# Modulation product of a 1-core transformer kernel: weighted sums on VectorE, partition sums by a column of ones on PE

## The reference, cut to what matters

```python
def swiglu(x, w_in, w_out):
    gate, up = jnp.split(x @ w_in, 2, axis=-1)
    return (jax.nn.silu(gate) * up) @ w_out

def modulate(h, shift, scale):
    return h * (1 + scale[:, None, :]) + shift[:, None, :]
```

## Time and profile before

| | us |
|---|---|
| median of 3 runs | 1971.3 |
| lowest and highest | 1969.5, 1971.41 |
| the profiled execution | 1973.3 |
| its span | 1971.1 |

### The profile page before, as it was taken

The page is one execution under the profiler, slowest core; times in us unless marked ns, Lnnn a source line. Parts: engine busy times, 40 slices in busy tenths (PEclk is TensorE's granted clock), DMA queues, the critical chain, the costliest instruction groups (busy, mean ns, idle before and its releaser), DMA issues.

```text
span 1971.1 us, 25483 instructions
## 1 busy us (share of the span) xinstructions
PE 1911.1 (97%) x10311; PEld 1589.6 (81%) x10311; DVE 1143.9 (58%) x1369; ACT 953.7 (48%) x1399; POOL 118.0 (6%) x182
## 2 busy tenths in 40 slices
PE   7999999999999999999999999899999999989997
PEld 5777788777777777877877777899889987878996
DVE  5554776645475445845556556675565557565554
ACT  4444563544454434544454445554554456544442
POOL 1400001000010000000010000000200001000000
PEclk9999999999999999999999999999999999999999
DMA  9867543876757675554586664444455545234552
GB/s 297 260 220 252 171 150 99 295 235 221 240 196 244 226 243 197 190 176 164 167 294 224 223 235 147 165 172 170 153 172 190 189 150 176 86 117 149 194 173 84
DMA packets 234100, 379.77 MB, mean 193 GB/s; under 512 B 12040, under 2 KB 152720, under 8 KB 233984
## 3 DMA queue, kind: packets, MB, share of 16 engines
q1 hardware_dynamic: 231200, 369.69, 56.2%
q0 software_dynamic: 2448, 8.33, 1.6%
q10 hardware_dynamic: 336, 0.14, 0.0%
HBM read 377.06 MB, written 1.05 MB: 192 GB/s over the span
## 4 chain that ended last, share of the span: by engine, by line
PE 89%; DVE 6%; ACT 2%; issue 1%; DMA 1%; POOL 1%; SPq 0%; POOLq 0%; ACTq 0%; DVEq 0%
PE ps L450 22%; PE ps L452 22%; PE ps L451 22%; PE ps L1134 4%; PE ps L1136 4%; PE ps L1137 4%; PE ps L460 4%; PE ps L577 2%; DVE w_lo L2047 2%; PE ps L627 1%; PE ps L1277 1%; PE ps L609 1%; PE ps L1256 1%; DVE xt_lo L2063 1%; ACT arena L1512 1%
## 5 line engine op out<-in xcount | busy, mean ns | idle before, releaser
L2047 DVE TENSOR_TENSOR w_lo<-raw,w_hi 128x1024 fp32r<-128x1024 f32 x602 | 719.9, 1227 | 241.7 <-ACT w_hi L1402 238.7
L1402 ACT ACTIVATE w_hi<-raw 128x1024 fp32r<-128x1024 f32 x602 | 614.6, 1056 | 258.0 <-PE ps L452 181.2
L450 PE MATMUL ps<-w_hi,xt_hi 128*128 128x512 f32 x1280 | 510.1, 398 | 16.2 <-DVE xt_lo L2197 11.8
L452 PE MATMUL ps<-w_hi,xt_lo 128*128 128x512 f32 x1280 | 500.4, 391 | 0.0
L451 PE MATMUL ps<-w_lo,xt_hi 128*128 128x512 f32 x1280 | 500.0, 391 | 0.0
L450 PE MATMUL ps<-w_hi,ht_hi 128*128 128x512 f32 x784 | 314.6, 401 | 5.9 <-DVE ht_lo L2225 2.7
L451 PE MATMUL ps<-w_lo,ht_hi 128*128 128x512 f32 x784 | 306.9, 391 | 0.0
L452 PE MATMUL ps<-w_hi,ht_lo 128*128 128x512 f32 x784 | 306.7, 391 | 0.0
L450 PEld LDWEIGHTS ps<-w_hi,xt_hi 128*128 128x128 f32 x1280 | 242.4, 189 | 68.1 <-issue 19.2
L452 PEld LDWEIGHTS ps<-w_hi,xt_lo 128*128 128x128 f32 x1280 | 242.3, 189 | 51.3
L451 PEld LDWEIGHTS ps<-w_lo,xt_hi 128*128 128x128 f32 x1280 | 242.6, 190 | 48.3 <-issue 1.2
(11 more groups left out here) (273 smaller groups left out, 1365.8 us busy)
## 6 DMA issues: line engine op xcount, KB each, us to landing
raw<-mlp_w_dram SPq DMA_DIRECT2D x192, 512.0 KB, 4.4
raw<-ffn_w_in_dram SPq DMA_DIRECT2D x176, 512.0 KB, 5.8
arena<-ada_w_dram SPq DMA_DIRECT2D x96, 512.0 KB, 6.5
raw<-ffn_w_out_dram SPq DMA_DIRECT2D x88, 512.0 KB, 4.5
raw<-odd_w_in_dram SPq DMA_DIRECT2D x48, 512.0 KB, 4.9
raw<-attn_w_qkv_dram SPq DMA_DIRECT2D x24, 512.0 KB, 4.9
raw<-even_w_in_dram SPq DMA_DIRECT2D x22, 512.0 KB, 4.7
raw<-ple_w_gate_dram SPq DMA_DIRECT2D x16, 512.0 KB, 4.5
```

The source lines that it names most:

```text
L450: pe.matmul(dst, a_hi, hi, start=start, stop=False)
L452: return pe.matmul(dst, a_lo, hi, start=False, stop=stop)
L1402: act.activation(w_hi[:, slot, c], raw[:, slot, c], ACT.Copy).then_inc(S(f"hi{slot}"), 1)
L2047: TT(w_lo[:, slot, c], raw[:, slot, c], w_hi[:, slot, c].bitcast(F32), ALU.subtract).then_inc(S(f"lo{slot}"), 1)
```

## The change

The slabs of the modulation weights are cut differently: 128 x 4 x 512 (half of the contraction, 512 columns) instead of 128 x 8 x 256, still 1 MB and 12 in a run. DVE now does the weighting: for each k and each of the two variants, `scalar_tensor_tensor` multiplies a 128 x 512 piece by a scalar for each partition (`s_col`) and adds it to a running sum `ada_sum` in `tmp` (the first k is a `tensor_scalar`). That is 8 DVE instructions a slab (`ada_part`, in two halves of 4), 384 in the program. After two slabs PE adds over the partitions (`ada_columns`): 8 float32 matmuls, each with a 128 x 128 piece of the sum as weights and a column of ones as the one moving column, which write straight into the columns that `ada_t` wants. There are 6 such groups in a run, after `up` in steps 1, 3, 5, 7 and 9, and one at the end in the place of `ada_turn`. `ada_product`, `ada_turn` and `ada_row` go; `ada_cols` becomes one copy.

DVE does slab 0 after the split that follows `gated(0)`, slabs 1 and 2 both in step 0, and slab i+2 in step i. SP loads slab 2 right behind slab 1, ahead of s5, and this load waits until DVE has done slab 0 (`ada_mac`).

```diff
...
@@ -344,13 +345,13 @@
             def ada_load(run, i):
 
-                g = ADA_STEPS * run + i
+                g = ADA_STEPS * run + (0, 1, 3, 4, 5, 6, 7, 8, 9, 10, 11, 2)[i]
                 if g >= 2:
 
-                    sp.wait_ge(S("ada_prod"), g - 1)
-                w = ada_slab(run, i)
+                    sp.wait_ge(S("ada_mac"), 8 * (g - 1))
+                w = ada_slab(run, g % ADA_STEPS)
...
                     ada_load(run, i + 1)
-                ada_load(run, FFN_STEPS)
+                    if i == 0:
+                        ada_load(run, FFN_STEPS)
                 load(wide(wo, 2 * FFN_STEPS - 2))
...
-            def ada_product(g):
...
-                for k in range(KT):
-                    q = 32 * (k % 4)
-                    last = pe.matmul(ps[q:q + 32, 7, 0:256], s_pad[:, k, 22 - 2 * i:54 - 2 * i], ada_raw[:, g % 2, k, :],
-                                     start=i == 0 and k < 4, stop=i == ADA_STEPS - 1 and k >= 4,
-                                     tile_position=(0, q), skip_group_check=True)
+            def ada_columns(group):
+
+                pe.wait_ge(S("ada_mac"), 16 * (group + 1))
+                for t in range(4):
+                    for v in range(2):
+                        c = 8 * (group % 6) + 2 * t + v
+                        last = pe.matmul(ps[:, 7, c:c + 1], ada_sum[:, group % 2, v, t * P:(t + 1) * P], ones[:],
+                                         start=True, stop=True)
                 last.then_inc(S("ada_prod"), 1)
...
                 for i in range(FFN_STEPS - 1):
                     hidden("f_", base + i, 2)
                     up(4, "f_up0")
-                    ada_product(ada + i + 1)
+                    if i % 2:
+                        if i == 1 and run:
+
+                            pe.wait_ge(S("ada_cols"), run)
+                        ada_columns(groups + i // 2)
...
-                ada_product(ada + FFN_STEPS)
...
-                ada_turn(run)
+                ada_columns(groups + 5)
...
-            def ada_row(run):
-                act.wait_ge(S("ada_prod"), ADA_STEPS * (run + 1))
-                act.activation(ada_rows[:], ps[:, 7, 0:256], ACT.Copy).then_inc(S("ada_row"), 1)
...
+            def ada_part(g, half):
+
+                if half == 0 and g % 2 == 0 and g >= 4:
+
+                    dve.wait_ge(S("ada_prod"), g // 2 - 1)
+                if half == 0:
+                    dve.wait_ge(S(f"ada_in{g % 2}"), 32 * (g // 2 + 1))
+                for j in (2 * half, 2 * half + 1):
+                    k = 4 * (g % 2) + j
+                    for v in range(2):
+                        to, w = ada_sum[:, g // 2 % 2, v, :], ada_raw[:, g % 2, j, :]
+                        n["ada"] += 1
+                        if k:
+                            dve.wait_ge(S("ada_mac"), n["ada"] - 2)
+                            ins = dve.scalar_tensor_tensor(to, w, s_col[:, v, k:k + 1], to, ALU.mult, ALU.add)
+                        else:
+                            ins = dve.tensor_scalar(to, w, s_col[:, v, k:k + 1], None, ALU.mult)
+                        ins.then_inc(S("ada_mac"), 1)
...
+                ada = ADA_STEPS * run
                 gated(base, out0)
                 split()
+                for half in range(2):
+                    ada_part(ada, half)
                 for i in range(FFN_STEPS - 1):
+                    slabs = (1, 2) if i == 0 else (i + 2,)
+                    ada_part(ada + slabs[0], 0)
                     ht_low(i)
                     split()
+                    ada_part(ada + slabs[0], 1)
                     split()
+                    for g in slabs[1:]:
+                        for half in range(2):
+                            ada_part(ada + g, half)
                     gated(base + i + 1)
...
```

More of the change, by code:

```diff
@@ L143, in build @@
         pt_lo = sb("pt_lo", [P, 2, SEQ], F32R)
-        s_pad = sb("s_pad", [P, KT, 54])
+        s_col = sb("s_col", [P, 2, KT])
+        ones = sb("ones", [P, 1])
         arena = sb("arena", [P, 15360])
@@ L226, in ada_slab @@
             w = rows(T["ada_w_2"][run // 2])
-            return w[:, :, bass.ds((run % 2) * 12 * 256 + i * 256, 256)]
+            return w[:, 4 * (i % 2):4 * (i % 2) + 4, bass.ds((run % 2) * 6 * 512 + i // 2 * 512, 512)]
         EVEN_CHUNKS = ((2048, 512), (2560, 256), (512, 512), (0, 512), (1024, 512), (1536, 512))
@@ L274, in build @@
         onorm_b = small[:, 128:256]
-        ada_rows = region(5120, 256)
-        ada_raw = region(10240, 2, KT, 256)
+        ada_raw = region(10240, 2, 4, 512)
+        ada_sum = cut(tmp[:], 2, 2, 512)
         pool_w = region(2560, KT, 256)
@@ L684, in ffn @@
                 base = FFN_STEPS * run
-                ada = ADA_STEPS * run
+                groups = ADA_STEPS // 2 * run
                 if out0 == 0:
@@ L1593, in ffn @@
                     act.activation(pt_hi[:], cut(bank(5), 2, SEQ), ACT.Copy).then_inc(S("pt_hi"), 1)
-                ada_row(run)
                 if run == 3:
@@ L2033, in _ @@
             ring = Ring()
-            n = {k: 0 for k in ("x", "x2", "sq", "epi", "pj", "ple", "step", "pool", "y", "mlp")}
+            n = {k: 0 for k in ("x", "x2", "sq", "epi", "pj", "ple", "step", "pool", "y", "mlp", "ada")}
             TT = dve.tensor_tensor
@@ L2181, in pool_add @@
                 dve.wait_ge(S("pool_y"), n["y"] + 1)
+                if n["y"] in (2, 3):
+                    dve.wait_ge(S("c_upd"), n["y"] - 1)
                 n["y"] += 1
                 c = slice(512 * half, 512 * half + 512)
-                t = cut(tmp[:], 2, MT, 512)[:, half, m]
+                if upd == "c_upd":
+                    t = arena[:, 8736 + 544 * half:8736 + 544 * half + 512]
+                else:
+                    t = cut(tmp[:], 2, MT, 512)[:, half, m]
                 TT(t, bank(b), gate[:, c], ALU.mult).then_inc(S("p_free"), 1)
@@ L2199, in ada_cols @@
             def ada_cols(run):
[L2201 to L2206, removed]
+                dve.wait_ge(S("ada_prod"), 6 * (run + 1))
+                dve.tensor_copy(ada_t[:, 2 * ADA_STEPS * run:2 * ADA_STEPS * (run + 1), :].rearrange("p t v -> p (t v)"),
+                                ps[:, 7, 0:48]).then_inc(S("ada_cols"), 1)
+            def ada_part(g, half):
[11 more added lines that the diff above has]
+                            ins = dve.scalar_tensor_tensor(to, w, s_col[:, v, k:k + 1], to, ALU.mult, ALU.add)
+                        else:
+                            ins = dve.tensor_scalar(to, w, s_col[:, v, k:k + 1], None, ALU.mult)
+                        ins.then_inc(S("ada_mac"), 1)
             def ffn(run, out0=4):
@@ L2276, in _ @@
             dve.wait_ge(S("silu_c"), 1)
-            dve.wait_ge(S("s_zero"), 1)
-            sil = small[:, 0:16].rearrange("p (v k) -> p k v", v=2)
-            dve.tensor_copy(s_pad[:, :, 22:24], sil).then_inc(S("s_set"), 1)
+            dve.memset(ones[:], 1.0)
+            step(dve.tensor_copy(s_col[:].rearrange("p v k -> p (v k)"), small[:, 0:16]))
             (s0, u0), (s1, u1) = ring.take(), ring.take()
@@ L2859, in _ @@
             step(pool.memset(minus_half[:], -0.5))
-            pool.memset(s_pad[:], 0.0).then_inc(S("s_zero"), 1)
             token_scale()
```

16 lines of the change are left out of this document (2 added, 14 removed).

## The result

The changed kernel takes 2001.9 us in the median, from 2001.7 to 2002.4; the kernel before 1970.4 beside it. The ratio is 1.016, with a 95% interval from 1.0143 to 1.0178: **slower by 31.5 us**, where 32.7 were forecast, and inside the range. The span grew from 1971.1 to 2000.3 us, less than the medians did, since the profiled execution before was 2.9 us over its median. Ratios here are estimated from all executions of both kernels and not from the two medians, so the two can differ by up to 0.001.

A forecast was written before the change was run, and what follows sets the result against it. PE, busy 97% of the span, was taken to set the pace. PE's account -5.5, step 0's DVE wait +29.4 and the clock +8.8 sum to +32.7 us, giving a median of 2004.0 us, range 1984 to 2019.

The forecast's parts named there:

- The term that decides, step 0: Step 0 of each run: 24 new DVE instructions ahead of gated(1) make PE wait at hidden(1), together 29.4 us lost.
- Its parts: Step 0's loss by run: 7.3 us in run 0, 7.8 in runs 1 and 2, 6.5 in run 3.
- PE's account: PE's own work over all runs: modulation products removed against column groups added, -5.5 us in sum.
- The clock term: Behind the four waits at hidden(1), PE falls to half clock: 4 x 2.2 = 8.8 us lost.
- It fits, so a delay of 2.6 us reaches nobody: Steps 1 to 9: DVE's 13.6 us fit in PE's 16.9 or 18.7, with split slabs a step ahead; no loss.
- PE's account alone: Rival: DVE gets through step 0 before PE reaches hidden(1), leaving only -5.5 us, 1965.8 us; chance 0.07.
- product 1 of each run: Modulation product in step 0, 1.21 us; its removal was counted inside step 0's term, not among the 38 products gained.
- the 1.0 us of run 3: Gain from removing product 0 in run 3, where a gate row stands behind it; counted inside step 0's term.

The follow-up runs named there:

- experiment 1: The changed kernel with slab 2 summed on DVE behind gated(1), SP's order as it is: 1990.3 us, ratio 1.0099.
- experiment 2: The changed kernel with slab 2 loaded behind s5 and s6, DVE's order as it is: 1998.1 us, ratio 1.0141.
- experiment 3: The changed kernel with slab 2 both summed behind gated(1) and loaded behind s5 and s6: 1979.1 us, ratio 1.0043.
- experiment 4: As experiment 3, with the second half of slab 1 also summed behind gated(1): 1977.9 us, ratio 1.0038.
- experiment 6: The changed kernel with no split or gated behind more than 4 sums (except s6's split), loads mostly in the earlier kernel's order: 1967.2 us, ratio 0.9987.
- experiment 11: The changed kernel with unused extra matmuls right behind step 0's own PE work, 54 in run 0, 40 in the others: 1998.7 us, ratio 1.0139.
- experiment 9: As experiment 6, with POOL's small loads and rope tables in run 0 started after up of step 3, not step 0: 1960.1 us, ratio 0.9945.
- experiment 5: The changed kernel with 34 unused extra matmuls of 384 columns on PE ahead of hidden(1) in each run: 2003.8 us, ratio 1.0173.

## Why the prediction was right

- **The term that decides, step 0, held:** +29.7 us measured, +29.4 forecast. Experiments 1 to 4 show its cause: with both orders turned and half a slab more moved, run 1's step 0 falls to 17.6 us. Most of it belongs to DVE's queue; the load's order counts for 3.8 us alone, and for 11.1 once DVE's is mended (1990.3 - 1979.1); DVE's order counts for 11.6 alone and 19.0 once the load's is mended.
- **Its parts were less even than forecast.** Run 1 lost 7.1 (7.8 forecast), run 2 6.8 (7.8), since s5 reached ACT 8.6 us after slab 2's issue and not 9.8. Run 3 lost 6.6 (6.5). Run 0 lost 9.1 (7.3): two errors that cancel in the sum. In run 0, slab 2's six sums took longer than in run 1, where the row above has 4.06:

```profile
51.22 5.63 DVE L2210 SCALAR_TENSOR_TENSOR tmp<-arena,s_col,tmp 128x512 f32<-128x512 f32 x6
```

- **PE's account held.** A group is 1.78 us (1.79 forecast), nine steps of experiment 6 gain 4.0 (3.7), and a pair of steady steps went from 36.11 to 35.46. Behind `hidden(1)`, runs 1 to 3 came out 0.7, 1.5 and 0.7 better than by account and clock together.
- **The clock was the mis-sized term:** 4 x 2.2 = 8.8 us forecast, 2.0 + 1.9 + 1.3 + 0 = 5.2 by experiment 11. The price of one loss held in runs 1 and 2. But run 3's step 1 lost less, and in run 0 the slow stretch lay under late loads, which made step 1 there 2.5 us longer by themselves. The runs show three losses of 1.3 to 2.0 us in the place of four of 2.2.
- **That the sum came within 1.2 us of the median's change is partly luck.** The clock term was 3.6 too large. In run 0's stretch behind `hidden(1)` the late loads took 2.5 us where 2.2 were put down to the clock. At the end of run 0 the clock stayed at 1.00 behind a wait of 3.11 us, where before it had been 0.70 and 0.73 over 6 us behind one of 2.68, which the account of that stretch did not hold.
- **"It fits, so a delay of 2.6 us reaches nobody" was the wrong step.** It did no harm to this forecast, because a long wait at `hidden(1)` lets every load catch up. Take that wait away and step 1 waits instead: 28 us of it in run 0, and the 1965 expected of experiment 4 missed by 13. Experiment 9 names the cause, POOL's stretch in run 0, which the prediction did not look at: its sum over DVE was one over averages, and loads had a fixed latency in it.
- **PE's account alone** was priced too low as a rival: without a wait at `hidden(1)` product 1 of each run and the 1.0 us of run 3 are gained too, -5.5 - 4 x 1.21 - 1.0 = -11.3. So it is luck that experiment 6, with the order mended, has 1967.2 beside the rival's 1965.8: its step 1 of run 0 still loses 6.5 us. Freed of POOL's work as well (experiment 9), 9.6 us are measured beside the 11.3.

Open stays how much of step 1's 28 us in run 0 is POOL's hold on DVE and how much its loads; experiment 9 moves both.

## What to carry to other kernels

Price the new work on an engine with room not by its share of busy time but in the one step where it piles up, ahead of the instruction that the bounding engine waits for. Put filler work behind what others wait for and in small pieces, and move the loads' order with it: either alone gave back 12 or 4 us, both 23. And cost a TensorE instruction with few moving columns at its weight load (0.111 us for 128 x 128 float32 here). Two single traces can differ by 1 to 3 us in a stretch because the clock fell behind a wait in one and not in the other, so look at the granted clock before putting such a difference down to the kernel.

## What the runs showed of the hardware

**SP's loads nearly stand still for 7 to 8 us, some 7 us after POOL starts its loads of tables** (2 to 512 KB each). The kernel before in slices of 1 us from 28 us on (share of the DMA engines in tenths, then GB/s), POOL's loads issued from 41.8 to 45.2 us:

```profile
DMA  0001999988999999999990009200899999999999
GB/s 0 0 0 24 291 311 376 348 264 233 345 384 373 369 382 372 350 348 377 371 61 0 10 22 2 0 0 8 324 372 397 339 374 392 404 381 354 353 349 347
```

Between 48 and 56 us hardly a byte moves, though SP has issued loads that have not landed: those of 40.5 to 47.2 us take up to 18.6 us to land. In experiment 9, where POOL issues them from 77.6 us on, the hole lies at 84 to 91 us. What in those loads does it was not tried.

**DVE is slower beside POOL.** In run 0, six sums take 5.63 us instead of 4.06, 0.94 instead of 0.68 each. In step 1 of run 0 four take 3.31 us beside POOL (experiment 6) and 2.73 with POOL's work moved away (experiment 9), two halves of a split 2.60 and 2.35. The Trainium skill, "SBUF — State Buffer", section "SBUF: two separate sides", says that a DVE instruction with two inputs in SBUF and a GpSimd instruction that reads SBUF lock one another out of a shared port pair. The rows agree: sums and splits have two such inputs and stretch, and `gated`, with one input in PSUM, takes 0.86 us beside POOL and 0.87 without. The two `tensor_scalar`, with one input in SBUF, stretch too, from 0.88 to 1.25 us; why was not tried.

**The length of a wait of 2 to 3 us does not tell whether the clock falls behind it.** The same wait of PE for `ht_low(10)` at the end of run 0, 3.11 or 3.12 us long, is in four traces, and so is the one of some 2.3 us at run 0's `hidden(0)`:

| wait, us | kernel | granted clock behind it |
|---|---|---|
| 3.11 | changed kernel | 1.00 |
| 3.12 | experiment 9 | 1.00 |
| 3.12 | experiment 6 | 0.73 and 0.70, 3 us each |
| 3.12 | experiment 11 | 0.50 and 0.52, 3 us each |
| 2.34 | changed kernel, experiment 6 | 1.00 over 4 us |
| 2.35, 2.37 | experiments 3 and 9 | 0.58, 0.63 over 4 us |

At `hidden(0)` it makes step 0 of run 0 18.4 us (experiment 9) instead of 16.9 (experiment 6), with the same instructions in it. Elsewhere the clock stayed up behind waits of 1.15 us (experiment 5, run 1), 2.45 and 2.53 (experiment 1, `hidden(1)` of runs 2 and 1), and fell behind 1.86 (experiment 5, run 2), 2.00 and 2.12 (`hidden(2)` of run 0, experiments 1 and 11). Behind each of the waits at `hidden(1)` in the changed kernel and in experiment 2, 5.2 us and longer, it was at 0.50 to 0.63 in the windows looked at. So one fall prices that case and says little of the next.
